# Copying the keys to both halves of the partitions, with one split step each and the low part of the attention keys on GpSimd

## The reference, cut to what matters

```
(c_b, c_c, c_x, q, k, v, iq, ik, iw, g_a, g_b) = jnp.split(h @ w_in[layer], PROJ_SPLITS, axis=-1)
dots = jnp.einsum("bthd,bsd->bths", iq_b, ik)
score = jnp.einsum("bth,bths->bts", iw_b, jax.nn.relu(dots))
score = jnp.where(causal[None], score, -jnp.inf)
_, idx = lax.top_k(score, k_top)
...
logits = jnp.einsum("bthd,btkd->bhtk", q_b, k_sel) * (HEAD_DIM ** -0.5)
logits = logits + moveaxis(rel_bias[rel_bucket(t_b[None, :, None] - idx)], -1, 1)
p = jax.nn.softmax(logits, axis=-1)
o = jnp.einsum("bhtk,btkd->bthd", p, v_sel)
```

## Time and profile before

| | us |
|---|---|
| median of 3 runs | 2690.65 |
| lowest, highest | 2688.7, 2692.6 |
| time of the profiled execution | 2683.23 |
| its span (first to last instruction) | 2681.4 |
| TensorE busy in it | 2521.8 |
| VectorE busy in it | 1708.9 |
| mean granted TensorE clock, of full speed | 0.976 |

### The profile page before, as it was taken

One profiled execution on the slowest core, in us unless ns is written; L12 is line 12 of the kernel. 1 busy time (PEld: TensorE's weight loads), 2 busy tenths in 40 slices (PEclk: granted clock), 3 DMA queues, 4 the chain that ended last, 5 costly groups with the idle time before them and its releaser, 6 DMA issues.

```text
span 2681.4 us, 31860 instructions
## 1 busy us (share of the span) xinstructions
PE 2521.8 (94%) x12136; PEld 2079.0 (78%) x12136; DVE 1708.9 (64%) x2896; ACT 970.5 (36%) x1749; POOL 633.3 (24%) x473
## 2 busy tenths in 40 slices
PE   5999999888999899999999989999999988999888
PEld 3778888677787688888888867888778767778877
DVE  5499999477424887886644378558676564009933
ACT  4431222477223332222411243333242254228732
POOL 2147522476543000000000220000000144324433
PEclk7999999999999999999999999999999989999999
DMA  4112233100455266564623222332364115232143
GB/s 166 44 37 67 79 94 98 48 1 17 162 172 146 87 189 194 174 187 135 228 79 110 67 91 87 105 100 79 102 259 149 52 51 173 79 103 71 44 146 102
DMA packets 260706, 293.17 MB, mean 109 GB/s; under 512 B 10856, under 2 KB 216140, under 8 KB 260556
## 3 DMA queue, kind: packets, MB, share of 16 engines
q1 hardware_dynamic: 260556, 291.14, 33.6%
HBM read 223.95 MB, written 66.10 MB: 108 GB/s over the span
## 4 chain that ended last, share of the span: by engine, by line
PE 64%; DVE 27%; ACT 5%; DMA 2%; issue 1%; POOL 1%; SPq 0%; DVEq 0%; ACTq 0%; POOLq 0%
PE ps L67 63%; DVE sm L100 6%; DVE m L97 6%; ACT tmp L73 2%; DVE tmp L103 2%; DVE tmp L79 2%; DVE sm L79 2%; PE ps L70 1%; DVE tmp L76 1%; DVE p2l L76 1%; ACT pth L73 1%; DVE wl L76 1%; DVE pwa L76 1%; DVE B2l L76 1%; DVE X L79 0%
## 5 line engine op out<-in xcount | busy, mean ns | idle before, releaser
L76 POOL TENSOR_TENSOR wl<-raw,wh 128x512 fp32r<-128x512 f32 (+1 forms) x224 | 292.9, 1329 | 1623.0 <-ACT wh L73 1622.9
L73 ACT ACTIVATE wh<-raw 128x512 fp32r<-128x512 f32 (+1 forms) x388 | 226.5, 621 | 256.5 <-PE ps L67 179.9
L73 ACT ACTIVATE tmp<-ps 128x512 f32<-128x512 f32 (+5 forms) x172 | 127.4, 751 | 391.3 <-PE ps L67 376.5
L67 PE MATMUL ps<-B2h,wh 128*128 128x512 f32 x616 | 244.0, 396 | 13.0 <-DVE B2l L76 6.7
L67 PE MATMUL ps<-B2h,wl 128*128 128x512 f32 x616 | 241.5, 392 | 0.0
L67 PE MATMUL ps<-B2l,wh 128*128 128x512 f32 x616 | 241.2, 392 | 0.0
L76 DVE TENSOR_TENSOR tmp<-tmp,ps 128x512 f32<-128x512 f32 x204 | 138.5, 685 | 107.5 <-PE ps L67 91.4
L67 PE MATMUL ps<-ah,wh 128*128 128x512 f32 (+1 forms) x608 | 191.9, 392 | 14.0 <-DVE xt L85 9.9
L73 ACT ACTIVATE wh<-ws 128x512 fp32r<-128x512 f32 x152 | 94.4, 626 | 290.8 <-DVE ws L76 263.6
L67 PE MATMUL ps<-B3h,wh 128*128 128x512 f32 x448 | 178.4, 398 | 16.6 <-DVE B3l L76 7.5
L67 PE MATMUL ps<-al,wh 128*128 128x512 f32 (+1 forms) x608 | 190.6, 390 | 0.0
(11 more groups left out here) (282 smaller groups left out, 5850.7 us busy)
## 6 DMA issues: line engine op xcount, KB each, us to landing
ada<-in_ada_w SPq DMA_DIRECT2D x48, 512.0 KB, 3.7
raw<-in_w_in SPq DMA_DIRECT2D x37, 512.0 KB, 4.5
raw<-in_a_w_in SPq DMA_DIRECT2D x33, 512.0 KB, 4.5
gates<-tmp SPq DMA_DIRECT2D x32, 512.0 KB, 3.0
raw<-in_w_ffn_gate SPq DMA_DIRECT2D x24, 512.0 KB, 6.0
hd<-tmp SPq DMA_DIRECT2D x22, 512.0 KB, 4.5
gf<-hd SPq DMA_DIRECT2D x22, 512.0 KB, 6.8
raw<-in_a_w_out SPq DMA_DIRECT2D x20, 512.0 KB, 3.5
```

What stands on the lines that cost most here:

```text
L67: return self.e.matmul(*a, **k) if self.e else Ins()
L73: return self.e.activation(*a, **k) if self.e else Ins()
L76: return self.e.tensor_tensor(*a, **k) if self.e else Ins()
```

## The change

It does four things.

- For each set of keys a second transfer is added, from `kt[0:64]` to `kt2[0:64]`, ahead of the one to `kt2[64:128]`. Both are issued by SP, one after the other. `kt2` then holds the keys in all 128 partitions.
- ScalarE makes the high part in one step over 128 partitions from `kt2`, once both copies have landed (one counter, `swap`, that both of them raise). The low part is one step over 128 partitions as well.
- The low part of set 1 moves from VectorE, where it stood behind `dve_scores`, to GpSimd, where it stands behind the low parts of the weights that `pool_w(e, "kv")` makes.
- The waits follow: the load of `T1` waits for GpSimd's counter (`plo`) in place of VectorE's, and the evacuation of the attention keys to `kt` waits until both copies of set 0 have landed.

```diff
 def sp_index / sp_qkv (i = 0 and 1)
+        e.dma_start(self.kt2[0:64, :], self.kt[0:64, :]).then_inc(self.sig["swap1"].up(("first", 1)), 16)
         e.dma_start(self.kt2[64:128, :], self.kt[0:64, :]).then_inc(self.sig["swap1"].up(("swap", 1)), 16)
         for j in range(4):
             self.sp_w(e, ("q", j))
             if j == 1:
                 e.wait_ge(*self.at("gst"))
-                e.wait_ge(*self.at("klo", 1, 1))
+                e.wait_ge(*self.at("klo", 1))
                 self.sp_table(e, "t1", self.T1, 0)
 def act_k_hi(self, e, i, after):
-        e.wait_ge(*self.at("kt%d" % i))
         for event in after:
             e.wait_ge(*self.at(*event))
-        e.activation(self.KH[0:64, :], self.kt[0:64, :], ACT.Copy).then_inc(self.sig["ahi"].up(("khi", i, 0)), 1)
         e.wait_ge(*self.at("swap", i))
-        e.activation(self.KH[64:128, :], self.kt2[64:128, :], ACT.Copy).then_inc(self.sig["ahi"].up(("khi", i, 1)), 1)
+        e.activation(self.KH[:, :], self.kt2[:, :], ACT.Copy).then_inc(self.sig["ahi"].up(("khi", i)), 1)
-    def dve_k_lo(self, e, i):
-        (two steps of 64 partitions)
+    def k_lo(self, e, i, signal):
+        e.wait_ge(*self.at("khi", i))
+        e.tensor_tensor(self.KL[:, :], self.kt2[:, :], self.KH[:, :].bitcast(F32), ALU.subtract).then_inc(
+            signal.up(("klo", i)), 1)
 def dve_qkv(self, e):
-        self.dve_k_lo(e, 1)
 def pool_qkv(self, e):
         self.pool_w(e, "kv")
+        self.k_lo(e, 1, self.sig["plo"])
         for j in range(4):
```

More of the change, by code:

```diff
@@ L1201, in sp_index @@
             e.wait_ge(*self.at(*event))
+        e.dma_start(self.kt2[0:64, :], self.kt[0:64, :]).then_inc(self.sig["swap0"].up(("first", 0)), 16)
         e.dma_start(self.kt2[64:128, :], self.kt[0:64, :]).then_inc(self.sig["swap0"].up(("swap", 0)), 16)
@@ L1253, in dve_index @@
             e.wait_ge(*self.at(*event))
-        self.dve_k_lo(e, 0)
+        self.k_lo(e, 0, self.sig["vlo"])
         e.wait_ge(*self.at("prod", "iw"))
@@ L1278, in pe_scores @@
             for j in range(4):
-                for event in (("iqh", j), ("iql", j), ("klo", 0, 0), ("klo", 0, 1)):
+                for event in (("iqh", j), ("iql", j), ("klo", 0)):
                     e.wait_ge(*self.at(*event))
@@ L1462, in sp_qkv @@
         e.wait_ge(*self.at("kt1"))
-        e.wait_ge(*self.at("klo", 0, 1))
+        e.wait_ge(*self.at("klo", 0))
+        e.dma_start(self.kt2[0:64, :], self.kt[0:64, :]).then_inc(self.sig["swap1"].up(("first", 1)), 16)
         e.dma_start(self.kt2[64:128, :], self.kt[0:64, :]).then_inc(self.sig["swap1"].up(("swap", 1)), 16)
@@ L1476, in act_qkv @@
         e.wait_ge(*self.at("prod", "kv"))
-        e.wait_ge(*self.at("klo", 0, 0))
+        e.wait_ge(*self.at("swap", 0))
         e.wait_ge(*self.at("prod", "iw"))
@@ L1609, in pe_attend @@
         pipeline(64, [(0, score), (4, turn), (6, lambda n: values(n, 1)), (5, lambda n: values(n, 0))])
-    KEYS1 = (("klo", 1, 0), ("klo", 1, 1))
+    KEYS1 = (("klo", 1),)
     def parts1(self, b):
```

## The result

The changed kernel took 2681.28 us in the median of 6 executions (2679.41 to 2685.61), the kernel before 2690.02 us beside it (2686.7 to 2692.6). The ratio is 0.9975, with a 95% interval of 0.9964 to 0.9986: faster by 0.25%, some 6.7 us (the two medians alone are 8.7 us apart), where the forecast was 2.3 us and a range from 2683.5 to 2693.0. Over those two sets it stands at 2683.3 us in the mean of 22, and the kernel before, over all sets on the chips of the experiments, at 2687.4 in the mean of 151: **4.1 us, with about 0.5 us of uncertainty**. That is nearly twice the forecast. The first set, with 6 executions of each, is not in these means; there the means are 8.3 us apart. One execution of the kernel before, 3200.2 us at a mean granted clock of 0.743, is in no mean.

The account below looks back on a forecast made before the run. TensorE, busy 2521.8 of 2681.4 us, was taken as the bound. The table gap -2.37, step overhead +0.05 and set 0 at 0 gave -2.3 us: 2690.65 to 2688.3 us, range 2683.5 to 2693.0.

Parts of the forecast that it names:

- The gap of 2.4 us at the flip: TensorE's idle time before the flip, waiting for the bias table: all that can be won, -2.37 us.
- The low part on GpSimd: Set 1's `KL` step: starts at 472.0, takes 2.35 us (bound 3.40), so the table's load goes out at 474.5.
- set 0 cost nothing: First key set, near 77 to 88 us: the later second copy stays hidden, 0; at the upper bound 0.3 us lost.
- nobody waits for VectorE between the search and the table's scaling: VectorE idle from 483.67 to 493.25: taking 4.70 us from it gives nothing by itself.
- the second copy: Added key transfer on SP's queue: lands 0.7 us later than the one copy did, bounds about 0.5 and 3.0 us.
- the margin of 7.0 us for the table: Table there at 480.8, wanted by TensorE at 487.83; margin 3.7 us with both upper bounds.
- The step that failed: Behind the flip, `q 2`, `q 3` and attention move as one piece, so the 2.3 us are kept to the end.
- The clock moves with the work: Rival: low-clock stretches around attention change in number; two fewer 2683.3 us (chance 0.12), two more 2693.3 us (0.10).
- the gap that goes did not lower the clock: Argument against the clock rival: clock 1.00 from 488 to 492, so no low stretch hangs directly on the gap.
- The table is late all the same: Rival: the table's load goes out after 481.5, so the change brings less or nothing, 2690.6 us; chance 0.06.
- set 0's copies hold up `iq 2`: Rival: TensorE waits at 87.45, costing the copies' lateness minus 2.7 us, 2690.4 us; chance 0.04.
- two tiles for `match_replace`: VectorE's search reads two SBUF tiles; by the skill's rule GpSimd's step waits or delays one by at most 2.35 us.

Follow-up runs that it names:

- those two sets: Two later sets of 11 executions each of the changed kernel, unedited, against the kernel before: ratios 0.9982 and 0.9985.
- e2: Kernel before with only set 1's low part moved to GpSimd, in two steps of 64 partitions, no second copy: ratio 0.9983, mean 2682.6 us.
- e3: Changed kernel with set 1's low part back on VectorE in one step, second copies kept: ratio to the kernel before 0.9985, mean 2683.0 us.
- e4: Changed kernel with the table's load held until GpSimd has made the low parts of `q 3`: ratio to the kernel before 1.0004, mean 2688.4 us.
- e6: Changed kernel with 11 more products (2.4 us of work) on TensorE ahead of the flip: ratio to the kernel before 0.9999, mean 2687.4 us.
- e16: Changed kernel with 11 more products (2.4 us) ahead of gate 8's projection, before attention: ratio to the kernel before 1.0004, mean 2688.0 us.
- e1: Kernel before, unedited, timed against itself: ratio 0.9996, mean 2686.9 us against 2687.7.
- e14: Kernel before, unedited, one more execution with a profile: 2687.68 us.
- e5: Changed kernel, unedited, timed again: ratio to the kernel before 0.9982, mean 2682.9 us.
- e15: Changed kernel, unedited, one more execution with a profile: 2679.98 us.
- e18: Changed kernel, unedited, timed once more as the zero for added work: ratio to the kernel before 0.9985, mean 2683.7 us.
- e17: Changed kernel with 11 more products (2.4 us) behind attention, ahead of the branches' fifth projection: ratio to the kernel before 0.9995, mean 2686.3 us.
- e9: Kernel before with 3 more products (0.65 us of work) between the flip's two parts: ratio 0.9996, mean 2686.3 us.
- e7: Changed kernel with 15 more products (3.3 us of work) on TensorE ahead of the flip: ratio to the kernel before 1.0000, mean 2687.7 us.
- e11: Kernel before with 8 more products (1.7 us of work) between the flip's two parts: ratio 1.0006, mean 2689.1 us.
- e12: Kernel before with 4 more products (0.9 us of work) between the flip's two parts: ratio 1.0007, mean 2688.8 us.
- e10: Changed kernel with 5 more products (1.1 us of work) between the flip's two parts: ratio to the kernel before 0.9993, mean 2684.8 us.
- e13: Kernel before with 17 more products (3.7 us of work) between the flip's two parts: ratio 1.0013, mean 2690.8 us.

## Why the prediction was wrong

**Right, and shown.** The gap of 2.4 us at the flip is the only thing that the change wins directly. It is closed by either half of the change (e2, e3), and holding the table back gives all of the gain away (e4). The low part on GpSimd took 2.41 us at 472.98 (forecast: 2.35 at 472.0), the table's load went out at 475.46 (474.5), the wait for the table is gone, `q 3` ended at 513.5 (513.4), and set 0 cost nothing: late by 1.1 us against a slack of 2.7. That nobody waits for VectorE between the search and the table's scaling held as well.

**A term mis-sized, without effect.** I took 0.7 us for the second copy; it was 1.1 to 1.25. SP needed 1.11 us for the two issues in set 1 and 1.58 in set 0, and a transfer of set 1 took 3.3 us in place of 3.0. It lay inside the bounds, and the margin of 7.0 us for the table (now about 6.4) took it.

**The step that failed** is the one behind the gap: "after the flip ... the start of attention, whose waits all count from the end of `q 3`. They move with it. So the 2.3 us are kept to the end." The waits do count from there, but the clock does not: in the profiles its fall comes 3.4 to 6.5 us after attention's start, and the stage behind it takes 170.3 to 174.3 us. Every kernel whose attention is held back by 2.3 to 2.9 us against the change, by an idle or a busy TensorE, at the flip or 120 us ahead of it, is 4.1 to 5.1 us slower in the mean (before, e4, e6, e16). In the profiles of those kernels (before, e1, e14, e4, e6, e16) the attention stage took 172.9 us in the mean, in those whose attention starts on time (after, e5, e15, e18, e2, e3, e17) 171.3. These 1.6 us, the gap's 2.3 and the 0.4 us for the clock's falls behind the gap make 4.3, and 4.1 were measured. That agreement is partly luck. The 1.6 us are uncertain by 0.7. And in the same thirteen profiles the stages behind attention took 2.1 us more in the late kernels as well, with 1.0 us of uncertainty (2.4 us of work taken off for e17), so that their spans are 6.3 us apart and not 4.1; the sum leaves this out.

So what is shown is that attention starting 2.3 to 2.9 us later costs 4.1 to 5.1 us, and that the length of the stage follows the stretch at the lower clock. That the one comes from the other is not shown, nor why late kernels land in the bad places more often: of six such profiles four are at 173.4 us or more, of seven on time none is. The tests that should have used it as a lever gave one hit (e9) and misses (e7, e11, e12), none of them clear of the noise. Profiles are one execution each.

Two more numbers on record speak against a full account by attention's place. First, other delays do not cost double: 1.2 us cost 1.5 (e10), 3.0 us cost 3.0 (e9), 3.3 us cost 4.4 (e7), 4.2 us cost 5.8 (e11) and 6.0 us cost 7.5 (e13), each over the change, with the gap of 2.3 us counted in where there is one. An excess of some 1.4 us on any delay, whatever its length (the mean of these with before, e4, e6 and e16), lies within about two uncertainties of each of them, so a costly place is not needed to explain them. Second, the mean granted clock of all executions is 0.9748 for the kernel before (151) and 0.9753 for the change (22). Among the executions of one kernel 0.001 less goes with 1.0 us more (a fit over all kernels, correlation 0.68), so by my estimate this difference is worth some 0.5 us, not 1.8. e18 has 0.9749, as e7 and e16 have (e6: 0.9748), and is 3.7 to 4.3 us faster than these. The cause of the second half stays open, and with it what share of it belongs to attention and what to the stages behind it.

**The rivals.** "The clock moves with the work" is the rival that came nearest, in its time (2683.3) and by the profiles of attention, though its mechanism is shown only in part. It was weighed at 0.12 for a gain, at two low stretches of 2.5 us, and argued against by "the gap that goes did not lower the clock". One execution could not tell that: in two of eight it does. I had taken the profiled execution of the kernel before for a typical one, and it is at the fast end: 2683.23 us against a mean of 2687.4, with attention in a cheap place (171.0 us). "The table is late all the same" and "set 0's copies hold up `iq 2`" did not happen.

The Trainium skill ("TensorE: Matmul & The Clock Gate", Part 1) says that the gate looks at TensorE's activity in windows that run free of the kernel. The table above agrees in this: executions of one kernel (before, e1, e14) have their falls 3.5, 3.9 and 4.4 us after the same product, and stay low for 10.2, 17.1 and 10.2 us.

The Trainium skill ("SBUF — State Buffer", Who interferes with whom) says that a VectorE instruction with two inputs in SBUF contends with a GpSimd instruction that reads SBUF. Here GpSimd's step beside `match_replace` took 2.41 us, against 2.39 for `ql` with VectorE idle. This is no case against the rule. The prediction counted two tiles for `match_replace`, but the trace has a step of its own that reads `m` ahead of each one:

```profile
472.89 0.07 DVE L100 MATCH_VALUE_LOAD sm<-m,sm 128x8 f32 x1
472.96 1.20 DVE L100 MATCH_REPLACE8 sm<-m,sm 128x1024 f32<-128x1024 f32 x1
```

So the long step may well have one input in SBUF, `sm`, and the rule's condition was then never met; the rows do not say which of the two tiles that they name it reads.

**Part of the miss** lies in the first set itself: 6.7 us by its ratio, 4.8 and 4.0 us by those of the later two (in means 8.3, 4.5 and 3.8). The mean of the later two sets, 2683.3 us, is only just below the range. The change is faster by 0.15 to 0.25%, around the bound of 0.2% that I had set.

## What to carry to other kernels

When a change takes a gap from TensorE ahead of a stage in which it works in short pieces, the gain need not be the gap alone. Here 2.3 us of gap were worth 4.1 us; that the stage is moved against the falls of the clock is the likeliest part of the rest, and not shown for all of it. Read such a stage in more than one execution, with the granted clock beside it, before saying what a shift is worth; a single profile showed neither the clock's fall at the gap nor the usual length of the stage. And test a gap with work of the same length in its place, at the gap and far ahead of it (e6, e16): that tells idleness from lateness, if the executions are enough for a difference of 2 us. The 11 of e6 alone were not.

## What was not expected of the hardware

- A step on 64 partitions took as long as one on 128: GpSimd's `kp` 2.40 us on 64x1024 and 2.41 on 128x1024, VectorE's 1.22 and 1.21, ScalarE's 1.06 and 1.06. Two half steps cost two full ones.
- VectorE's `kp` step took 3.32 us beside GpSimd's `ql` in the kernel before, and 1.21 us in e3, where it started 0.04 us before GpSimd's, which then took 3.41: only the one that came second was long.
- Executions of one kernel on one chip spread over 8 to 9 us (2683.0 to 2691.8 in 33 executions of the kernel before), far more than what most small edits are worth.
